# Sliding-window attention: softmax diagonals built by GpSimd instead of ScalarE, and the next projection's weight halves made one by one between the block pairs

## The reference, cut to what matters

```python
scores = jnp.einsum('bnqhgd,bnkhd->bnhgqk', qb, kb).astype(jnp.float32) * (ATT_HEAD_DIM ** -0.5)
scores = jnp.where(mask[None, :, None, None], scores, -jnp.inf)
probs = jax.nn.softmax(jnp.concatenate([scores, sink], axis=-1), axis=-1)[..., :-1]
out = jnp.einsum('bnhgqk,bnkhd->bnqhgd', probs.astype(v.dtype), vb)
```

## Time and profile before

| quantity | value |
|---|---|
| median of 3 runs | 2988.07 us (2984.94 to 2988.78) |
| the profiled execution, own time | 2990.42 us |
| span of its instructions | 2988.7 us |
| mean granted TensorE clock | 0.968 of full speed |
| PE busy | 92% |
| DVE, POOL, ACT busy | 56%, 46%, 31% |
| the sliding attention's products, outputs and low halves | about 1588 to 1644 us of the span |
| the GLA level loop behind it | about 1644 to 1690 us |

### The profile page before, as it was taken

How to read it: one execution, slowest core, us unless ns; L and a number is a source line. 1 busy time by engine, 2 the same in 40 slices (tenths; PEclk the granted TensorE clock), 3 DMA queues, 4 the chain that set the end, 5 groups by cost and what they waited for, 6 DMA issues and landing times.

```text
span 2988.7 us, 32920 instructions
## 1 busy us (share of the span) xinstructions
PE 2761.2 (92%) x12322; PEld 2097.8 (70%) x12322; DVE 1667.0 (56%) x3130; ACT 929.1 (31%) x1696; POOL 1372.9 (46%) x995
## 2 busy tenths in 40 slices
PE   7989999999999999999896789999999899989944
PEld 6856888777888678888776668888888654434421
DVE  1033144565335254330306648999896999856686
ACT  3275334555333332322335232111112940000001
POOL 3433543766446133444342235444445854444465
PEclk9999999999999999999998899999999999999978
DMA  4311232112234136654230036999999369999998
GB/s 155 102 56 36 84 100 85 57 37 77 92 137 132 50 115 201 198 176 106 78 93 29 8 120 235 365 388 393 374 391 402 122 228 383 388 411 410 409 386 299
DMA packets 218799, 590.69 MB, mean 198 GB/s; under 512 B 24193, under 2 KB 48914, under 8 KB 218130
## 3 DMA queue, kind: packets, MB, share of 16 engines
q1 hardware_dynamic: 137312, 301.22, 29.5%
q0 software_dynamic: 75968, 275.81, 24.4%
q10 hardware_dynamic: 5362, 11.56, 1.2%
HBM read 576.98 MB, written 7.35 MB: 196 GB/s over the span
## 4 chain that ended last, share of the span: by engine, by line
PE 69%; DVE 12%; DMA 10%; POOL 3%; issue 3%; ACT 3%; SPq 0%; POOLq 0%; DVEq 0%; ACTq 0%
PE ps L1795 15%; PE ps L1290 13%; PE ps L1291 13%; PE ps L1292 13%; DMA rows<-in_v,expert 5%; DMA rows<-in_u,expert 5%; DVE ps L2496 3%; POOL wlo L1080 1%; PE ps L1388 1%; POOL rows L1201 1%; PE ps L1256 1%; PE ps L1823 1%; DVE rows L2482 1%; PE ps L1473 1%; PE ps L1475 1%
## 5 line engine op out<-in xcount | busy, mean ns | idle before, releaser
L1080 POOL TENSOR_TENSOR wlo<-wraw,whi 128x1024 fp32r<-128x1024 f32 x258 | 627.8, 2444 | 869.9 <-ACT whi L578 869.4
L578 ACT ACTIVATE whi<-wraw 128x1024 fp32r<-128x1024 f32 x258 | 269.3, 1058 | 712.2 <-PE ps L1292 605.3
L1290 PE MATMUL ps<-hhi,whi 128*128 128x512 f32 x1096 | 433.9, 396 | 21.1 <-DVE hlo L1960 6.0
L1835 PE MATMUL ps<-stream,hg 128*128 128x512 f32 x1024 | 442.4, 595 | 8.2 <-DMA stream<-in_v 8.2
L1795 PE MATMUL ps<-haff,stream 128*128 128x256 f32 x2048 | 444.1, 380 | 2.2 <-ACT stg L984 2.2
L1291 PE MATMUL ps<-hlo,whi 128*128 128x512 f32 x1096 | 430.9, 393 | 0.0
L1292 PE MATMUL ps<-hhi,wlo 128*128 128x512 f32 x1096 | 430.4, 393 | 0.0
L1795 PEld LDWEIGHTS ps<-haff,stream 128*128 128x128 f32 x2048 | 390.1, 191 | 55.7 <-ACT stg L984 2.4
L1201 POOL DMA_INDIRECT rows<-in_u,expert x256 | 265.4, 1037 | 263.8 <-DVE hid L2482 137.3
L1835 PEld LDWEIGHTS ps<-stream,hg 128*128 128x128 f32 x1024 | 195.3, 191 | 255.2 <-issue 245.4
L1201 POOL DMA_INDIRECT rows<-in_v,expert x256 | 250.2, 977 | 261.2 <-DVE ps L2496 122.9
(11 more groups left out here) (464 smaller groups left out, 4490.4 us busy)
## 6 DMA issues: line engine op xcount, KB each, us to landing
stream<-in_ut SPq DMA_DIRECT2D x128, 512.0 KB
stream<-in_v SPq DMA_DIRECT2D x128, 512.0 KB
wraw<-in_w_in SPq DMA_DIRECT2D x96, 512.0 KB
wraw<-in_w_ada SPq DMA_DIRECT2D x48, 512.0 KB
wraw<-in_w_gu SPq DMA_DIRECT2D x88, 256.0 KB
wraw<-in_w_down SPq DMA_DIRECT2D x22, 512.0 KB
wraw<-in_w_br_ssm SPq DMA_DIRECT2D x16, 512.0 KB
wraw<-in_w_xkv SPq DMA_DIRECT2D x16, 512.0 KB
```

What stands on the lines that cost most here:

```text
L578: act.activation(whi[:, n % WSLOTS, 0:kn, :], wraw[:, n % WSLOTS, 0:kn, :], ACT.Copy).then_inc(w_hi, 1)
L1080: pool.tensor_tensor(wlo[:, n % WSLOTS, 0:kn, :], wraw[:, n % WSLOTS, 0:kn, :], whi[:, n % WSLOTS, 0:kn, :].bitcast(F32), ALU.subtract).th ...
L1290: pe.matmul(dst, lh, rh, start=k == 0, stop=False)
L1835: ins = pe.matmul(ps[:, 2 * i + half, :], hg[:, n, P * i:P * i + P], stream[j][:, 4 * half:4 * half + 4, :], start=n == 0, stop=n == NKEYS ...
```

## The change

ACT no longer makes the diagonals. POOL makes them, four heads to an instruction (the identity, broadcast over four heads, times four columns of `srec`, broadcast over 128 columns), two instructions a block, each adding 4 to `sw_p`. ACT's rounding of out0's four chunks is taken out of `group(G["in4"], ...)`; one chunk is rounded after line 933 of each block, ahead of `gla_part(b)`. POOL makes one low half behind each block's diagonals, `q_in` moves behind the second of these, and `k_out` and the `gl_q` stay behind all four. DVE waits, before it overwrites `srec`, until POOL has read it for the block before.

```diff
-            def group(g, jobs, evac):
-                round_upto(ahead(GROUPS[g][2]))
+            def group(g, jobs, evac, rounds=True):
+                if rounds:
+                    round_upto(ahead(GROUPS[g][2]))
...
-            def sw_diagonals(b):
-                act.wait_ge(s("sw_rec"), b + 1)
-                if b:
-                    act.wait_ge(s("sw_tr"), 4 * b)
-                for h in range(SW_HEADS):
-                    act.activation(sw_dg[:, h, :], ident, ACT.Copy, scale=srec[:, h:h + 1]).then_inc(s("sw_p"), 1)
-
             sw_exp(0)
             for b in range(NT):
-                sw_diagonals(b)
                 if b == 0:
-                    group(G["in4"], (0, 1), to_tokens(gv_s, 0))
+                    group(G["in4"], (0, 1), to_tokens(gv_s, 0), rounds=False)
...
                 act.activation(hhi[:, 0:4, P * b:P * b + P], b4(4), ACT.Copy).then_inc(s("sw_ohi"), 1)
+                round_upto(GROUPS[G["in4"]][2] + b + 1)
                 gla_part(b)
...
             after("dn1")
-            after("in4")
-
-            pool.wait_ge(s("gla_act"), 2)
-            pool.tensor_tensor(q_in[:], q_in[:], gq_t[:], ALU.mult).then_inc(s("qin_ready"), 1)
+            def sw_diagonals(b):
+                pool.wait_ge(s("sw_rec"), b + 1)
+                if b:
+                    pool.wait_ge(s("sw_tr"), 4 * b)
+                for h in range(0, SW_HEADS, 4):
+                    pool.tensor_tensor(sw_dg[:, h:h + 4, :], ident.unsqueeze(1).to_broadcast([P, 4, P]),
+                                       srec[:, h:h + 4].unsqueeze(2).to_broadcast([P, 4, P]), ALU.mult).then_inc(s("sw_p"), 4)
+
+            last = GROUPS[G["in4"]][2]
+            rest_upto(last)
+            for b in range(NT):
+                sw_diagonals(b)
+                rest_upto(last + b + 1)
+                if b == 1:
+                    pool.wait_ge(s("gla_act"), 2)
+                    pool.tensor_tensor(q_in[:], q_in[:], gq_t[:], ALU.mult).then_inc(s("qin_ready"), 1)
             pool.wait_ge(s("gla_act"), 4)
             pool.tensor_tensor(k_out[:], k_out[:], gk_t[:], ALU.mult).then_inc(s("kout_ready"), 1)
...
                 link(v.tensor_tensor(sden, st[:, 16:24], st[:, 24:32], ALU.add))
+                if b:
+                    v.wait_ge(s("sw_p"), SW_HEADS * b)
                 v.reciprocal(srec, sden).then_inc(s("sw_rec"), 1)
```

## The result

The changed kernel's median is 2993.93 us, against 2985.80 for the kernel before, eleven runs each; the ratio is 1.0025 with a 95% interval of 1.0016 to 1.0034. So the change costs 8.1 us (4.8 to 10.1 by the interval), where 9.3 to 9.4 were forecast. The median was forecast at 2997.5 us and is 3.6 lower: 1.3 of that is the smaller cost, and 2.3 is that the kernel before has a median of 2985.80 over eleven runs, and not the 2988.07 of its first three. The spans of the two profiled executions are 2993.9 and 2988.7 us.

A forecast was written before the change was run, and what follows sets the result against it. The prediction took the stage as bound by TensorE waiting for one diagonal after another, with GpSimd's in-order queue late after the change. Terms -5.9 + 3.3 + 2.75 + 7.55 + 1.6, +0.1 more: +9.4, 2997.5 us; range 2990.5 to 3002.5.

The forecast's parts named there:

- The port: Block 0: VectorE and GpSimd share ports, so low halves slow the GLA decays; without them the second reciprocal comes 7.8 us earlier.
- alone the three are worth 4.7 us, with gaps 4.9: VectorE's three GLA decay steps in block 0, without GpSimd's low halves beside them: 4.9 us with gaps, against 12.9 us.
- The first hand-over: Block 0 to 1: block 1's diagonal products start at 1600.9 instead of 1606.79, -5.9 us, behind GpSimd's low half and diagonal.
- Block 2: Rounding, low half, `q_in` and diagonal stand ahead of its products, at 1618.6; gives back 3.3, gain down to -2.6 us.
- block 3: Rounding, low half and diagonal ahead of its products, at 1633.8 against 1633.65: gives back 2.75, leaving +0.15 us.
- the end: Behind block 3, the fourth low half delays `k_out` and the first `gl_q`; `level_difference(2)` starts +7.7 us later, a 7.55 term.
- The collision: Level loop: the second `gl_q` takes the port, so `level_difference(2)` ends 2.1 us later; the next loses 0.5 less; +1.6.
- The opening gain carries: Faster rival, 6%: diagonals 2 and 3 start at their reciprocals, the level loop catches up, -5.9 us remains, 2982.2 us.
- One sign of being right: POOL's diagonals of blocks 2 and 3 start at the end of `q_in` or a low half, 5 us or more behind the reciprocal.
- Carried, but the end is paid: No-change rival, 14%: blocks 2 and 3 keep their 5.9 us, the end costs 7.7 + 1.6; +3.4, 2991.5 us.
- More ports, slower clock: Slower rival, 12%: diagonals take 1.91 us, TensorE starts slow, or the first hand-over gains nothing; +14 to +15, 3002.5 us.
- What costs nothing: ScalarE's freed 9.8 us gives no gain; VectorE's extra wait for `sw_p`, SP's later loads and later `q_in` cost nothing.

The follow-up runs named there:

- the run that freed the ports alone: Kernel before, with GpSimd's four low halves moved from block 0 to behind the seven `gl_q`; 2987.53 us, ratio 0.9999.
- the run with the new order: Changed kernel, GpSimd's queue reordered: each low half behind a later block's diagonals or behind `gl_q`, never between a reciprocal and its diagonals; 2975.79 us, ratio 0.9961.
- The run with the last half late: Changed kernel, with GpSimd's fourth low half behind all seven `gl_q` instead of ahead of `k_out`; 2984.85 us, ratio to before 0.9997.
- the runs with another order: Changed kernel, low halves moved behind later diagonals or `gl_q`: 2975.79 us; that with `q_in` behind all `gl_q`, chunk 2's half behind the second: 2971.06 us.
- the kernel with the new order and the diagonals on ScalarE: Kernel before, ScalarE's roundings moved as in the change, diagonals left on ScalarE, GpSimd's low halves reordered behind later blocks or `gl_q`; 2982.07 us, ratio 0.9979.

## Why the prediction was right

The median, 2993.93 us, is inside the range, moved in the direction forecast (+8.1 us), and by the mechanism forecast. That +8.1 is so near to +9.4 is in part luck: the stage itself cost 6.8 us in the traces, 2.5 less than the sum had for it, near the low end of its bounds (+6.3 to +14). The 1.3 us between the traces and the medians are within the interval and have no cause on record.

*The port.* The step "alone the three are worth 4.7 us, with gaps 4.9" came out at 1.22 + 0.70 + 2.63 with gaps 4.6, and the run that freed the ports alone shows the cause. By the rule of the Trainium skill that the prediction names (SBUF — State Buffer, Who interferes with whom), that the one that comes second waits for the whole instruction of the first, the traces agree, also for the smallest operations: in the run with the new order 0.17 us became 1.55 for 8 columns. The second reciprocal came 8.1 us earlier against the first (7.8 forecast).

*The first hand-over*, -5.9: measured -6.0. It was set by GpSimd's low half and not by VectorE, as said.

*Block 2*, forecast to give back 3.3, gave back 2.8; *block 3* gave back 2.1 instead of 2.75; *the end* cost 6.3 instead of 7.55. The hand-overs are right: from line 933 (now 926) to the next products 7.4 us (7.6 forecast) and 5.1 (5.25), and to `level_difference(2)` 8.6 (8.75 and 0.05). The mis-sized term is TensorE's own time. I had kept block 3's products at 6.41 us and put block 2's at 0.8 above 5.44; they took 5.36 and 5.78. Lengths of products after a wait were treated as if the wait fixed them. Over all runs of this study the same 32 matmul records took 3.81 to 6.69 us. With block 1's (5.84 instead of 6.19) this is 0.35 + 0.46 + 1.05 = 1.9 of the 2.5 us between +9.3 and +6.8; the hand-overs, 0.15 to 0.2 shorter each, are the rest.

*The collision* at the second `gl_q`: forecast as 3.35 us for `level_difference(2)` with 0.5 taken off the next, sum +1.6; measured 3.36, then 2.24 instead of 2.61, sum +1.7. The run with the last half late has 1.22 there.

*The slack rivals.* "The opening gain carries" had a test: does the third diagonal start at its reciprocal? It started 5.7 us behind. One sign of being right was put too strongly: block 3's diagonals were to start 5 us or more behind their reciprocal too, and started 3.4 us behind. The prediction's own terms give only 3.6 (0.5 + 1.05 + 0.1 + 2.36 + 0.05 us from line 933, less some 0.5 from there to the reciprocal, as in its block 2). Yet the runs with another order show that the mechanism of this rival exists, and that its price was named too low: when nothing stands ahead of the diagonals the gain is 11 to 16 us. "Carried, but the end is paid" failed at its first half: blocks 2 and 3 gave back 4.9 of the 6.0 us. "More ports, slower clock" did not come as a cost: no diagonal took more than 1.04 us, and over the products of blocks 1 to 3 the granted clock was 0.64, 0.64 and 0.70, where it had been 0.60, 0.69 and 0.58. TensorE did start the level loop slowly, as the bounds allowed for (3.68 us at a granted clock of 0.53, and not 2.06, for its first level products), but beside the `level_difference(2)` of 3.36 us, so that it added nothing.

*What costs nothing.* SP's later loads stayed invisible: out1's first low half starts at +124.24 before and at +131.06 after, later by the stage's own 6.8 us. So did the extra wait of VectorE: in the change VectorE's third and fourth reciprocals start within 0.05 us of the end of the addition ahead of them.

One flaw of form: the sum in the text gives both +9.3 and +9.4, and the forecast was made with the second.

## What to carry to other kernels

When work moves to an engine that runs in order, price the place in its queue before the instruction: the first diagonals cost 1.04 us, the rounding and the low half ahead of them 1.05 + 2.35. Filling work belongs behind the urgent instruction and should take inputs that were ready a round earlier; the same instructions so ordered turned a loss of 8 us into a gain of 16. And before an operation is called slow, look at what GpSimd does beside it.

## What the runs showed of the hardware that was not expected

An operation on 128x8 elements with two inputs in SBUF waits for a 2.36 us instruction of GpSimd just as a big one does: 1.55 us instead of 0.17, twice in one run and on its chain of waits. One input is enough in another operation: the change of sign of the maxima, 128x8 elements, takes 0.17 us alone, 0.97 beside a diagonal instruction in the changed kernel, and 2.29 beside a `gl_q` in the kernel with the new order and the diagonals on ScalarE:

```profile
1613.81 2.29 DVE L2269 TENSOR_SCALAR stat<-stat 128x8 f32<-128x8 f32 x1
...
1613.71 2.36 POOL L1185 TENSOR_TENSOR gl_q<-gl_d,gq_t 128x1024 f32<-128x1024 f32 x1
```

GpSimd pays too: in six runs the instruction that follows the last `gl_q` at once, a low half or `q_in`, took 3.34 to 3.36 us instead of 2.36, beside VectorE's last product of level keys.

The 32 matmul records of one block's diagonal products took 3.81 us at a granted clock of 1.00 and 6.69 us at 0.55:

```profile
1627.50:1634.20 6.70, 6.69 (x32) 6.50 (x32) 0.69 (x1) 1.19 (x2) 0.85 (x1) 0.55 0.20 76
```

In both cases with a wait of 1.89 us the clock was 1.00 (3.81 us), but after one of 1.46 us it was 0.73 (5.14 us), after one of 2.42 us 0.69 (5.44 us), and a wait of 2.60 us gave 3.81 us once and 5.31 us once. The other 24 groups, with waits of 2.90 to 9.18 us, took 5.23 to 6.69 us. So shortening a wait of TensorE can pay twice, but the second payment could not be forecast from the wait alone; what else decides it was not settled.
